# Sixteen gate units of the first layer as joined 512-column products

## The reference, cut to what matters

```
h = concat(meta_tokens, x)                       # 16 + 256 token rows, 1024 features
hn = h * rsqrt(mean(h*h) + eps) * norm_g
proj = hn @ w_in                                 # 5128 columns
u_pool, z_pool, q, k, v, z_attn, f_logit, g_pool, g_attn = split(proj)
...
merged = sigmoid(g_pool) * (y_pool @ w_up_pool) + sigmoid(g_attn) * (y_attn @ w_up_attn)
x = (h + merged @ w_out)[after the 16 meta rows]
```

## Time and profile before

| | us |
|---|---|
| median of three runs | 1202.51 |
| the profiled execution | 1202.38 |
| its span | 1200.4 |
| outside the span | 1.98 |
| PE busy | 1192.8 (99%) |
| DVE busy | 934.4 (78%) |
| ACT busy | 728.5 (61%) |
| gate units on PE, with the two pool units | about 101.9 to 148.3 |

### The profile page before, as it was taken

The page is one execution under the profiler, slowest core; times in us unless marked ns, Lnnn a source line. Parts: engine busy times, 40 slices in busy tenths (PEclk is TensorE's granted clock), DMA queues, the critical chain, the costliest instruction groups (busy, mean ns, idle before and its releaser), DMA issues.

```text
span 1200.4 us, 22410 instructions
## 1 busy us (share of the span) xinstructions
PE 1192.8 (99%) x7964; PEld 1100.4 (92%) x7964; DVE 934.4 (78%) x1619; ACT 728.5 (61%) x1201; POOL 90.6 (8%) x104
## 2 busy tenths in 40 slices
PE   9999999999999999999999999999999999999998
PEld 9899999888888999999888889988888999888887
DVE  7566788988876789788988867888876777888853
ACT  7455656666664589476666655666654566666642
POOL 5851000000000001610000000000000000000000
PEclk9999999999999999999999999999999999999999
DMA  8444655555564344114555743555664323555730
GB/s 327 180 142 153 210 209 181 195 193 196 214 241 154 133 175 161 69 36 165 193 203 180 257 162 120 205 198 177 221 235 151 132 106 115 203 199 184 253 133 35
DMA packets 47991, 209.86 MB, mean 175 GB/s; under 512 B 3350, under 2 KB 4772, under 8 KB 43444
## 3 DMA queue, kind: packets, MB, share of 16 engines
q1 hardware_dynamic: 46720, 204.96, 48.6%
q10 hardware_dynamic: 1204, 4.01, 1.0%
HBM read 207.86 MB, written 1.10 MB: 174 GB/s over the span
## 4 chain that ended last, share of the span: by engine, by line
PE 92%; DVE 5%; ACT 2%; issue 1%; DMA 0%; DVEq 0%; ACTq 0%
PE main L2128 25%; PE main L2130 13%; PE main L2440 13%; PE main L2101 8%; PE main L2102 8%; PE main L2103 8%; PE main L2442 7%; DVE w_lo L1132 2%; PE side L2234 1%; PE main L2599 1%; PE main L2483 1%; PE side L2208 1%; PE side L2483 1%; PE main L2774 1%; PE main L2776 1%
## 5 line engine op out<-in xcount | busy, mean ns | idle before, releaser
L1132 DVE TENSOR_TENSOR w_lo<-raw,w_hi 128x1024 fp32r<-128x1024 f32 (+3 forms) x365 | 466.2, 1285 | 8.4 <-ACT w_hi L577 7.3
L2128 PE MATMUL main<-xs,w_hi 128*128 128x512 f32 x1328 | 461.0, 390 | 0.1
L577 ACT ACTIVATE w_hi<-raw 128x1024 fp32r<-128x1024 f32 (+2 forms) x363 | 402.3, 1110 | 73.9 <-PE main L2103 58.6
L2130 PE MATMUL main<-xs,w_lo 128*128 128x256 f32 x1328 | 374.5, 282 | 0.0
L2128 PEld LDWEIGHTS main<-xs,w_hi 128*128 128x128 f32 x1328 | 249.2, 188 | 52.5 <-DVE w_lo L1132 0.4
L2130 PEld LDWEIGHTS main<-xs,w_lo 128*128 128x128 f32 x1328 | 251.0, 189 | 0.0
L2440 PE MATMUL main<-h_both,w_hi 128*128 128x512 f32 x682 | 236.6, 390 | 0.0
L2442 PE MATMUL main<-h_both,w_lo 128*128 128x256 f32 x682 | 192.3, 282 | 0.0
L2440 PEld LDWEIGHTS main<-h_both,w_hi 128*128 128x128 f32 x682 | 128.0, 188 | 26.8
L2442 PEld LDWEIGHTS main<-h_both,w_lo 128*128 128x128 f32 x682 | 128.9, 189 | 0.0
L2101 PE MATMUL main<-xs,w_hi 128*128 128x256 f32 x368 | 105.4, 286 | 0.0
(11 more groups left out here) (479 smaller groups left out, 1887.2 us busy)
## 6 DMA issues: line engine op xcount, KB each, us to landing
raw<-in_w_gu_a SPq DMA_DIRECT2D x44, 1024.0 KB, 5.1
raw<-in_w_gu_b SPq DMA_DIRECT2D x44, 1024.0 KB, 5.2
raw<-in_w_down_a SPq DMA_DIRECT2D x16, 1408.0 KB, 6.0
raw<-in_w_down_b SPq DMA_DIRECT2D x16, 1408.0 KB, 6.1
raw<-in_w_in SPq DMA_DIRECT2D x15, 1024.0 KB, 7.6
raw<-in_w_in_a SPq DMA_DIRECT2D x13, 1024.0 KB, 5.2
raw<-in_w_gates SPq DMA_DIRECT2D x4, 1024.0 KB, 5.2
raw<-in_w_up SPq DMA_DIRECT2D x4, 1024.0 KB, 5.3
```

The costliest lines, as they stand in the source:

```text
L577: act.activation(w_hi[:, u % RING, 0:n], raw[:, s % RAW, u % 2, 0:n], ACT.Copy).then_inc(hi_ready, 1)
L1132: return dve.tensor_tensor(dst, src, hi.bitcast(F32), ALU.subtract)
L2128: pe.matmul(bank[:, :], piece(w_hi, u, k), xs[:, k], start=k == 0, stop=k == KC - 1, skip_group_check=True)
L2130: ins = pe.matmul(bank[:, 0:SEQ], piece(w_lo, u, k), xs_hi[:, k], start=False, stop=k == KC - 1, skip_group_check=True)
```

## The change

The sixteen gate units are computed in the manner of `project_halves`, with `xg[:, :, k, META:TOK]` as the 512 columns (two runs of 256 columns, one row of parts apart). ACT copies the second half of each bank into the gate's place in SBUF, DVE adds the first half and then multiplies by `rstd` in place. The copy stands in ACT's loop behind the slots and the squares; DVE waits for it (`low_half`) where its evacuation stood, and its multiply waits for its own addition. The sigmoids wait for the multiply (`normed`). The semaphores `low_half` and `normed` are those of the feed-forward blocks, whose counts start 16 higher (`first_half`).

```diff
@@ ACT @@
+                if u >= 24:
+                    act.wait_ge(unit_used, in1_unit(u) + 1)
+                    act.activation(gates[:, u % 8, (u - 24) // 8, :], main[(t0 + u - 1) % 4][:, SEQ:2 * SEQ], ACT.Copy)\
+                       .then_inc(low_half, 1)
                 if u == 33:
-                    act.wait_ge(evac, t0 + 31)
+                    act.wait_ge(normed, 8)
...
-            act.wait_ge(evac, FIRST_TILE["up"])
+            act.wait_ge(normed, 16)
@@ DVE @@
-                    taken(dst, t, scale).then_inc(evac, 1)
+                    if u < 24:
+                        taken(dst, t, scale).then_inc(evac, 1)
+                    else:
+                        dve.wait_ge(low_half, u - 24 + 1)
+                        dve.tensor_tensor(dst, main[t % 4][:, 0:SEQ], dst, ALU.add).then_inc(evac, 1)
+                        dve.wait_ge(evac, t + 1)
+                        dve.tensor_tensor(dst, dst, scale, ALU.mult).then_inc(normed, 1)
@@ PE @@
+                elif u >= 24:
+                    bank = bank_of(t0 + u - 1)
+                    unit_begin(in1_unit(u))
+                    for k in range(KC):
+                        pe.matmul(bank[:, :], piece(w_hi, in1_unit(u), k), xg[:, :, k, META:TOK], start=k == 0,
+                                  stop=k == KC - 1, skip_group_check=True)
+                        ins = pe.matmul(bank[:, 0:SEQ], piece(w_lo, in1_unit(u), k), xg_hi[:, k, META:TOK], start=False,
+                                        stop=k == KC - 1, skip_group_check=True)
+                    unit_end(ins)
```

More of the change, by code:

```diff
@@ L440, in first_half @@
         def first_half(which):
-            return 2 * FT * FFNS.index(which) - (2 * FFN_FIRST["b1"] if which == "b1" else 0) \
+            return 16 + 2 * FT * FFNS.index(which) - (2 * FFN_FIRST["b1"] if which == "b1" else 0) \
                 - (2 * FFN_FIRST["b1"] + 4 if which == "b2" else 0)
```

## The result

The changed kernel takes 1209.11 us, median of six runs (1208.92 to 1209.42), against 1202.47 us for the kernel before (six runs): ratio 1.0055, 95% interval 1.0045 to 1.0065. That is 6.6 us slower; 1208.7 us was forecast, and the range was 1206.6 to 1211.0. The profiled execution took 1209.18 us with a span of 1207.4 us.

A forecast was written before the change was run, and what follows sets the result against it. PE, busy 99%, was taken as the bound. Waits of 6.59 us less 0.43 gained made 6.16 us; 1200.4 + 6.2 = 1206.6 us span, 1208.5 with 1.98 around it, median 0.13 above: 1208.7 us, range 1206.6 to 1211.0.

The forecast's parts named there:

- The gain in the matmuls: Gate stage, PE: joined pairs save one instruction start in three, 0.027 us a unit, 0.43 us for all sixteen.
- the walk: Gate stage: PE, DVE and ACT queues in program order with durations from the trace; puts unit 42 6.16 us later.
- The waits: Gate stage: PE waits for late `w_lo` before nine units because DVE waits for ACT's copy, 6.59 us in all.
- the ring: From u = 30, squares wait for DVE additions, which wait for copies behind squares: 3.12 us a round against a 2.77 unit.
- the rival without any wait of a square: Gate stage: squares never wait for DVE's additions; the walk then loses 3.1 us, 1205.6 us in all; chance 0.08.
- The tail: Behind the gates: first `gated` 1.4 us later than PE's delay, absorbed by DVE's idle time, so costed at 0.
- The capacity: Up stage: DVE's idle time that can take up the late first `gated`, 0.54 + 6 x 0.21 = 1.8 us.
- No wait: Rival, gate stage: the ring of four units takes up the copy everywhere, giving 1202.1 us; chance 0.06.
- The ring doesn't bind: Rival, gate stage: a square never waits for an addition, so the loss is 3.1 us, 1205.6 us; chance 0.08.
- Cheaper columns: Rival, matmuls: 512 columns cost less, a pair 0.1 us shorter; time about the forecast's, or 1190 without waits; chance 0.01.
- More is lost behind: Rival, behind the gates: tail not absorbed or ring drifts further, 8.5 to 11 us lost, 1211 to 1213.5; chance 0.08.

The follow-up runs named there:

- pairs_alone: Kernel before with only the matmuls joined in pairs; DVE evacuates with one multiply, ACT copies nothing, the second bank half isn't read: 1202.10 us (ratio 0.9997).
- the triples: Two runs of the changed kernel with three 256-column matmuls a block, third into the second bank half, differing in one start flag: 1209.29 and 1209.22 us.
- copy_after_slot: Changed kernel with ACT's copy moved right behind `w_hi` in all sixteen turns, ahead of silus, `y_hi` and squares: 1204.12 us (ratio 1.0013).
- sigmoids_last: Changed kernel with ACT's copy first in its turn and both sigmoids done behind the last gate: 1203.47 us (ratio 1.0007).
- copy_early_24_27: Changed kernel with ACT's copy moved behind `w_hi` in turns 24, 25 and 27 alone: 1206.28 us (ratio 1.0031).
- copy_first: Changed kernel with ACT's copy put ahead of `w_hi` in each turn, the work unchanged: 1202.17 us (ratio 0.9996 against the kernel before).
- copy_before_square: Changed kernel with ACT's copy put just ahead of the square in turns 28 to 35: 1207.22 us (ratio 1.0039 against the kernel before).

## Why the prediction was right, point by point

**The gain in the matmuls**, costed at 0.43 us: 0.42 in pairs_alone. The two separate runs of columns cost nothing. The prediction took this from the 390 ns of the earlier trace rows, which is a duration and not a distance between starts; it is pairs_alone that shows it. With nothing saved the prediction gave two values, 0.43 us more by the sum and 0.1 more by the walk (6.3 for 6.16); the triples give 0.1, the walk's.

**The waits**, costed at 6.59 us. The same sum from the starts of the changed kernel (distance between two starts, less the usual 0.12, plus what the second matmul is late):

| before unit | forecast | measured |
|---|---|---|
| 27 | 0.58 | 0.79 |
| 28 | 0.28 | 0.29 |
| 30 | 0.99 | 1.06 |
| 33 (pool) | 0.57 | 0.68 |
| 34 | 0.86 | 0.82 |
| 35 | 0.29 | 0.27 |
| 38 | 0.77 | 0.90 |
| 39 | 1.90 | 1.96 |
| 40 | 0.35 | 0.40 |
| sum | 6.59 | 7.17 |

The nine places are right and no other is found. The 7.17 us are more than the 5.0 us of idle time, because a matmul's recorded duration runs on over the start of the next one: before unit 27 the idle time is 0.56 us, but 0.71 us too much lie between the starts.

The sum was 0.6 us short. A part is the hand-over from ACT's copy to DVE's addition, taken as 0.04 us from the earlier trace rows: here the addition at 139.62 starts 0.11 us after the copy's end at 139.51. The copy itself is 0.03 us shorter than costed, so that from start to start it is 0.47 us (139.15 to 139.62) against 0.43 in the walk, 0.04 us on each such path. At unit 27 it is 0.50 (108.70 to 109.20), 0.07 more. The rest of the 0.2 us there is ACT's way to the copy: from the start of `w_hi` over the table load and the silu to the next instruction it takes 3.34 us (105.36 to 108.70), as it did before the change (105.16 to 108.50), where the walk had 3.25 (105.1 to 108.35). What is left at the other units, up to 0.1 us each, isn't traced. With 0.35 to 0.42 us saved, 7.17 gives the stage's 6.82 us or a little less. The medians differ by 6.64.

**The causes.** Two were taken away alone. The silus, `y_hi` and its wait for `y1`: 2.9 us (6.82 - 3.88). The copy's place behind the squares, which closes the ring: 2.2 us (6.82 - 4.59); the rival without any wait of a square had 3.1 us less than the forecast, which this order doesn't reach since the squares still wait. Both together, in copy_after_slot, 5.2 us. That this is close to 2.9 + 2.2 is partly chance: the wait in the second pool unit (0.68 us) is gone in either run and so stands in both figures, while copy_after_slot brings the wait before unit 39 from 1.96 down to 1.21 us, which neither of the two does. The 1.6 us that remain there are waits of 0.43, 0.40 and 1.21 us before units 34, 35 and 39, less the 0.4 saved. In the changed kernel the sigmoid wasn't taken away by itself; its share there is read from ACT's timeline, and with the copy first it is the 0.18 us of sigmoids_last. With the copy first no recorded wait is left. That a square waits for DVE only because the gate work stands before it was argued from the queues; L591 waiting for L1165 after the change, and for nothing on DVE before it, agrees with this.

**The tail**, costed at 0: 1.40 us late as worked out, and no wait of PE. The capacity was put at 1.8 us; sigmoids_last measures 2.1.

**The rivals.** "No wait" was close at the place it named: the `w_lo` made after unit 24 has 3.8 us of slack and comes 4.3 us later than before, counted from the start of the stage (111.22 - 102.14, against 106.66 - 101.91). But that place doesn't decide: in copy_early_24_27 this wait is gone and 3.88 us are lost all the same. The rival's time is reached by copy_first. "The ring doesn't bind" fell with copy_before_square. "Cheaper columns" fell with pairs_alone: a 512-column matmul takes 0.23 us from start to start here too (104.41 to 104.64 in the changed kernel). The 131 ns of the Trainium skill (TensorE: Matmul & The Clock Gate, Back-to-back issue gap) were not seen in any run. "More is lost behind" fell with the second stretch above, which is full, and the 49.29 us against 49.30.

**What stays open.** Whether copy_first is faster than the kernel before: the profile says 0.25 us in the stage, the medians 0.37, and the interval holds 1. How the 7.2 us divide between the causes: they overlap, as said, so the figures above are what each order of the queue saves and not shares of a sum.

## What to carry to other kernels

A new short instruction is priced by what stands ahead of it in its queue and by what stands behind the instruction that waits for it, not by its duration: against pairs_alone, the same sixteen copies with their additions and multiplies lengthen the stage by 7.2 us behind the silus and squares and by 0.2 us at the head of the turn. Before a helper engine is put between the end of a product and the next weights, write down the turns of both engines in order with durations and look for rings; a ring whose round (3.2 us) is longer than the unit (2.8 us) makes PE wait though, over the stage, ACT is idle for 40% of the time and DVE for 28%. Here it closed in three of the sixteen turns, and opening it saved 2.2 us. In a stream of float32 products in parts, joining two of three matmuls saved 0.026 us a unit here (0.42 over sixteen), less than the shortest of the nine waits.

## What the runs showed of the hardware beside this

- Three matmuls of 256 columns and a 512-column one with one of 256 differ by 0.42 us over 128 blocks, 3.3 ns a block of about 350: with the same 768 streamed columns in both, the number of matmuls counts for 1%.
- The hand-over from an ACT copy to a waiting DVE addition took 0.10 to 0.14 us in the gate stage of the changed kernel (139.51 to 139.62, 109.06 to 109.20) and 0.03 in the feed-forward block (302.63 to 302.66).
- When PE had waited for a `w_lo`, its matmul started 0.14 us after the end of the `w_lo` in the changed kernel (111.22 to 111.36, 146.39 to 146.53), and the next one came 0.08 us later than usual (0.31 us instead of 0.23).
- A stage's start in one profiled execution scatters by 0.57 us (101.82 to 102.39) between kernels with equal work before it. Lengths of stages are the better measure.
